# Reordering the front and the end of the state-space mixer of a three-part model kernel

## The reference, cut to what matters

```python
proj = hn @ w_in                                   # z 2048, xbc 3072, dt 64
z, xbc, dt_raw = jnp.split(proj, [SSD_INNER, SSD_INNER + SSD_XBC], axis=-1)
xbc = silu(depthwise_conv_centered(xbc, conv_w, conv_b))       # 5 taps over the tokens
xs, bm, cm = jnp.split(xbc, ...)                   # x 2048, B 4x128, C 4x128
dt = softplus(dt_raw.reshape(b, s, 2, 32) + dt_bias)
log_a = dt * -exp(a_log)                           # two directions, 32 heads
y = bidir_scan(cm, bm, xs * dt_f, xs * dt_b, log_a_f, log_a_b)  # chunks of 128
y = (y + xs * d_skip) * silu(z)
y = y * rsqrt(mean(y*y over each of 4 groups) + EPS) * norm_g
out = y @ w_out                                    # 2048 -> 1024
```

## Time and profile before

| | |
|---|---|
| median of 3 runs | 991.22 us (990.34 to 992.37) |
| profiled execution | 990.58 us, its span 988.2 us, mean granted TensorE clock 0.998 |
| TensorE (PE) busy | 954.5 us, 97% |
| ScalarE (ACT), VectorE (DVE), GpSimd (POOL) busy | 62%, 48%, 69% |
| DMA | 177.64 MB, mean 180 GB/s |
| the state-space mixer | about 342 to 548 us of the span |

### The profile page before, as it was taken

The page is one execution under the profiler, slowest core; times in us unless marked ns, Lnnn a source line. Parts: engine busy times, 40 slices in busy tenths (PEclk is TensorE's granted clock), DMA queues, the critical chain, the costliest instruction groups (busy, mean ns, idle before and its releaser), DMA issues. The chain is left out here.

```text
span 988.2 us, 15848 instructions
## 1 busy us (share of the span) xinstructions
PE 954.5 (97%) x6053; PEld 834.4 (84%) x6053; DVE 478.6 (48%) x1022; ACT 609.2 (62%) x1150; POOL 677.1 (69%) x538
## 2 busy tenths in 40 slices
PE   6999999999999999999998999999999999999998
PEld 5888768999999797888877799999997887788787
DVE  4734655444434545876844554444345231233652
ACT  7635668555455676977967764555566555775641
POOL 5986736857566686787778586657776964865664
PEclk9999999999999999999999999999999999999999
DMA  9684525775554657447456366565556538734221
GB/s 335 232 235 150 170 86 180 247 241 193 185 174 168 181 143 206 161 148 247 170 177 219 121 208 213 171 213 171 173 170 204 151 127 274 244 119 159 97 86 43
DMA packets 124952, 177.64 MB, mean 180 GB/s; under 512 B 13185, under 2 KB 86797, under 8 KB 124685
## 3 DMA queue, kind: packets, MB, share of 16 engines
q1 hardware_dynamic: 120701, 168.91, 52.4%
q10 hardware_dynamic: 4176, 7.71, 2.3%
HBM read 175.47 MB, written 5.24 MB: 183 GB/s over the span
## 5 line engine op out<-in xcount | busy, mean ns | idle before, releaser
L533 POOL TENSOR_TENSOR wlo<-raw,whi 128x512 fp32r<-128x512 f32 (+1 forms) x502 | 656.9, 1343 | 282.8 <-ACT whi L1254 266.8
L550 PE MATMUL PS<-Th,whi 128*128 128x256 f32 (+2 forms) x968 | 275.2, 285 | 0.8 <-DVE arena L1871 0.7
L552 PE MATMUL PS<-Th,wlo 128*128 128x256 f32 (+2 forms) x968 | 272.3, 282 | 0.0
L551 PE MATMUL PS<-Tl,whi 128*128 128x256 f32 (+2 forms) x968 | 272.3, 282 | 0.0
L1254 ACT ACTIVATE whi<-raw 128x1024 fp32r<-128x1024 f32 (+1 forms) x144 | 150.7, 1047 | 152.9 <-PE PS L552 113.7
L547 PE MATMUL PS<-whi,Th 128*128 128x512 f32 (+1 forms) x512 | 203.1, 397 | 10.1 <-DVE Tl L1848 7.3
L1871 DVE SCALAR_TENSOR_TENSOR arena<-PS,cols,arena 128x255 f32<-128x255 f32 (+1 forms) x272 | 118.6, 478 | 186.6 <-ACT arena L1388 160.9
L549 PE MATMUL PS<-whi,Tl 128*128 128x512 f32 (+1 forms) x512 | 197.1, 385 | 0.0
L548 PE MATMUL PS<-wlo,Th 128*128 128x512 f32 (+1 forms) x512 | 196.8, 384 | 0.0
L550 PEld LDWEIGHTS PS<-Th,whi 128*128 128x128 f32 (+2 forms) x968 | 184.0, 190 | 6.7 <-DVE arena L1871 3.1
L551 PEld LDWEIGHTS PS<-Tl,whi 128*128 128x128 f32 (+2 forms) x968 | 184.0, 190 | 1.8 <-issue 0.7
(11 more groups left out here) (250 smaller groups left out, 1034.6 us busy)
## 6 DMA issues: line engine op xcount, KB each, us to landing
raw<-in_ffn_w_up_dram SPq DMA_DIRECT2D x44, 1024.0 KB, 5.1
raw<-in_w_in_dram SPq DMA_DIRECT2D x23, 1024.0 KB, 5.3
raw<-in_ffn_w_down_dram SPq DMA_DIRECT2D x22, 1024.0 KB, 4.9
raw<-in_c_w_in_dram SPq DMA_DIRECT2D x16, 1024.0 KB, 5.3
raw<-in_ab_w_in_dram SPq DMA_DIRECT2D x14, 1024.0 KB, 7.4
raw<-in_c_w_out_dram SPq DMA_DIRECT2D x8, 1024.0 KB, 5.1
raw<-in_ab_w_out_dram SPq DMA_DIRECT2D x4, 1024.0 KB, 5.3
raw<-in_c_w_in_dram SPq DMA_DIRECT2D x8, 512.0 KB, 5.4
```

Source lines behind the costliest of these rows:

```text
L533: i = nc.gpsimd.tensor_tensor(lo_of(n)[:, c:e], raw[n % NRAW][:, c:e], hi_of(n)[:, c:e].bitcast(F32), ALU.subtract)
L550: mm(o, wh, ah, start=first, stop=False)
L551: mm(o, wh, al, start=False, stop=False)
L552: return mm(o, wl, ah, start=False, stop=last)
```

## The change

On TensorE, `dt_T` moves into the middle of the slot bc(0); `run_sums` moves from the middle of the second z slot to the middle of xs(0,1); the second z slot runs token tile by token tile, with a semaphore after the first; in `turned_x` of the first group the wait for the gate is by tile; `last_turn(1)` moves from before `out_last` into it, behind its first six products. On ScalarE, softplus comes ahead of the first centre taps with `ssd_rate` under the same Exp; the Ln, the exponential and the sums' copy come ahead of the last centre taps; weights' high parts move with them; the gate's SiLU runs by tile between the conv's SiLUs; in the last group one `high` goes behind the gate and one (`high(b + 5)`) ahead of `exps(4)`. On VectorE the softplus comes ahead of the first taps, its result stays in PSUM (`sp`) and is read there by the steps to `lnd` and `la`, with one more copy to SBUF. On GpSimd, in the last group, the first four `kept` come one slot earlier.

```diff
@@ -405,7 +405,8 @@
         sums_before, kept_before = {}, {}
         for g in range(SG):
             b = slot_no[(("bc", g + 1), 0)] if g + 1 < SG else slot_no[("mo1", 0)]
-            for u, k, m in ((0, 5, 4), (2, 5, 4), (4, 7, 5), (6, 7, 5)):
+            first = 4 if g + 1 < SG else 3
+            for u, k, m in ((0, 5, first), (2, 5, first), (4, 7, 5), (6, 7, 5)):
                 sums_before.setdefault(b + k, []).append((g, u))
                 kept_before.setdefault(b + m, []).append(8 * g + u)
@@ -986,8 +987,11 @@
                 def turned_x():
                     pe.wait_ge(*at("cv", (g, 1)))
-                    pe.wait_ge(*(at("s_m", (g - 1, 3)) if g else read((("z", 0), 1))))
+                    if g:
+                        pe.wait_ge(*at("s_m", (g - 1, 3)))
                     for t in range(NT):
+                        if not g:
+                            pe.wait_ge(*read((("z", 0), t)))
                         for j in range(4):
                             i = tr(PS[:, 4 + t, j * P:(j + 1) * P], cvb[:, j, t * P:(t + 1) * P], ident)
                     i.then_inc(*done("s_xt", g))
@@ -1042,7 +1046,6 @@
                 tile_diag(1)
                 if last:
                     ssd_slot(g + 1, 5, mid=lambda: last_turn(0))
-                    last_turn(1)
             def run_sums():
                 pe.wait_ge(*at("la"))
@@ -1055,17 +1058,26 @@
                         i = mm(PS[0:32, 7, P * k:P * k + P], dtt[:, 2 + c, 32 * r:32 * r + 32], cc(("le", "ge")[r]), start=True, stop=True)
                 i.then_inc(*done("sums"))
-            ssd_slot(0, 0)
-            pe.wait_ge(*at("dt_row"))
+            def steps_T():
+                pe.wait_ge(*at("dt_row"))
+                for t in range(NT):
+                    i = tr(PS[:, 7, S + 64 * t:S + 64 * t + 64], dtr[:, t * P:(t + 1) * P], ident[0:64, 0:64])
+                i.then_inc(*done("dt_T"))
+
+            ssd_slot(0, 0, mid=steps_T)
+            ssd_slot(0, 1)
+            ssd_slot(0, 2, mid=run_sums)
+            n = slot_no[(("z", 0), 1)]
+            pe.wait_ge(*low(n))
+            h, w = hi_of(n), lo_of(n)
             for t in range(NT):
-                i = tr(PS[:, 7, S + 64 * t:S + 64 * t + 64], dtr[:, t * P:(t + 1) * P], ident[0:64, 0:64])
-            i.then_inc(*done("dt_T"))
-            ssd_slot(0, 1)
-            ssd_slot(0, 2)
-            slot_tm((("z", 0), 1), 4, 4, False, True, mid=run_sums)
+                for k in range(4):
+                    i = three(PS[:, 4 + t, :], h[:, k * 512:(k + 1) * 512], w[:, k * 512:(k + 1) * 512],
+                              Th[:, 4 + k, t * P:(t + 1) * P], Tl[:, 4 + k, t * P:(t + 1) * P], False, k == 3, True)
+                i.then_inc(*(done("w_used", n) if t else done("sum", (n, 0, 1))))
             for g in range(SG):
                 ssd(g)
-            out_last("mo1", 8, (4, 6), by_tile=[("T_lo", ("yl", 0)), ("T_lo", ("yl", 1))])
+            out_last("mo1", 8, (4, 6), mid=lambda: last_turn(1), by_tile=[("T_lo", ("yl", 0)), ("T_lo", ("yl", 1))])
             ffn(1)
@@ -1409,13 +1421,19 @@
                 act.wait_ge(*at("t5_sum"))
                 act.dma_start(t5s.rearrange("(h k) -> h k", h=16), t5r).then_inc(*done("t5_src", 0, 16))
-            def softplus(key, neg, n):
+            def ssd_rate():
+                act.wait_ge(*at("load_ssd"))
+                act.activation(dtt[:, 5, :], dtt[:, 5, :], ACT.Exp).then_inc(*done("ssd_a"))
+
+            def softplus(key, neg, n, also=None):
                 spx = spxs[key]
                 act.wait_ge(*at("sp_x", key))
                 act.activation(spx[1], spx[0], ACT.Abs).then_inc(*done("sp_abs", key))
                 act.wait_ge(*at("sp_abs", key))
                 act.activation(spx[2], spx[1], ACT.Exp, scale=-1.0).then_inc(*done("sp_exp", key))
+                if also:
+                    also()
                 act.wait_ge(*at("sp_u", key))
                 act.activation(spx[4], spx[3], ACT.Ln).then_inc(*done("sp_ln", key))
@@ -1548,8 +1566,8 @@
                     act.activation(cvb[:, 2 * j + m, :], PS[:, xbc_bank(g, j), m * S:(m + 1) * S], ACT.Identity,
                                    scale=col("cw2", ch), bias=col("cb", ch)).then_inc(*done("c_ctr", (g, 2 * j + m)))
-            def ssd_silu(g):
-                for j in (2, 0, 1):
+            def ssd_silu(g, js=(2, 0, 1)):
+                for j in js:
                     act.wait_ge(*at("c_cnv", (g, j)))
                     act.activation(cvb[:, 2 * j:2 * j + 2, :] if j < 2 else bct[g % 2][:, :, :], cvb[:, 2 * j:2 * j + 2, :],
                                    ACT.Silu).then_inc(*done("cv", (g, j)))
@@ -1572,7 +1590,8 @@
                         i = act.activation(o, crow[v % 4][:, k, :], ACT.Exp, bias=ncs[:, a:a + 1])
                     i.then_inc(*done("s_e", (g, u)))
-                high(b + 1)
+                if more:
+                    high(b + 1)
                 if g:
                     act.wait_ge(*at("w_used", slot_no[(("z", g), 1)]))
                     copy_block(("z", g), zt[g % 2], 0, func=ACT.Silu)
@@ -1600,6 +1619,8 @@
                 exps(3)
                 if more:
                     ssd_centre(g + 1, 1, False)
+                else:
+                    high(b + 5)
                 exps(4)
                 exps(5)
                 high(b + 5)
@@ -1637,25 +1658,31 @@
                 act.wait_ge(*at("s_ss", (g, 1)))
                 sqrt_of(("s", g), st[:, 98:100], st[:, 96:98], 512)
+            def gate_tile(t):
+                act.wait_ge(*(at("w_used", slot_no[(("z", 0), 1)]) if t else at("sum", (slot_no[(("z", 0), 1)], 0, 1))))
+                act.activation(zt[0][:, t, :], PS[:, 4 + t, :], ACT.Silu).then_inc(*done("read_a", (("z", 0), t)))
+
             used(("dt", 0), ahead=False)
             act.activation(dtr, PS[0:64, 6, 0:S], ACT.Copy).then_inc(*done("dt_row"))
+            high(split_at(slot_no[(("bc", 0), 0)], 2))
+            softplus("ssd", False, 128, also=ssd_rate)
             ssd_centre(0, 2)
-            softplus("ssd", False, 128)
-            act.wait_ge(*at("load_ssd"))
-            act.activation(dtt[:, 5, :], dtt[:, 5, :], ACT.Exp).then_inc(*done("ssd_a"))
-            ssd_centre(0, 0)
-            ssd_centre(0, 1)
             act.wait_ge(*at("la"))
             act.activation(lnd, lnd, ACT.Ln).then_inc(*done("lnd"))
+            ssd_centre(0, 0, False)
+            high(split_at(slot_no[(("xs", 0), 0)], 3))
             act.wait_ge(*at("cums"))
             act.activation(dtt[:, 8:10, :], PS[:, 6, 0:128].rearrange("p (a b) -> p a b", a=2), ACT.Exp).then_inc(*done("ex"))
             act.wait_ge(*at("sums"))
             act.activation(csum, PS[0:32, 7, :], ACT.Copy).then_inc(*done("csum"))
             act.wait_ge(*at("csum"))
             act.dma_start(csr.rearrange("c r h t -> h (c r) t"), csum.rearrange("h (a t) -> h a t", a=4)).then_inc(*done("csr_out", 0, 16))
-            ssd_silu(0)
-            act.wait_ge(*at("w_used", slot_no[(("z", 0), 1)]))
-            copy_block(("z", 0), zt[0], 4, func=ACT.Silu)
+            ssd_centre(0, 1, False)
+            ssd_silu(0, (2, 0))
+            gate_tile(0)
+            ssd_silu(0, (1,))
+            gate_tile(1)
+            high(split_at(slot_no[(("xs", 0), 1)], 3))
             for g in range(SG):
                 ssd(g)
             post_norm(2, ("mo1", 7), "ffn1", 0)
@@ -2200,12 +2227,14 @@
                     last_scale(0)
                 ssd_tile(g, 1)
+            sp = spxs["ssd"][7]
+            softplus("ssd", 128, sp)
+            ts(lnd, sp, 1e-37, None, ALU.max)
+            nc.vector.tensor_copy(dtt[:, 0:2, :].rearrange("p a b -> p (a b)"), sp)
+            dve.wait_ge(*at("ssd_a"))
+            stt3(out=dtt[:, 2:4, :], in0=sp.rearrange("p (a b) -> p a b", a=2), scalar=-1.0, in1=bc(dtt[:, 5, :], 1, 2),
+                 op0=ALU.mult, op1=ALU.mult).then_inc(*done("la"))
             ssd_conv(0, 2)
-            softplus("ssd", 128, dtt[:, 0:2, :].rearrange("p a b -> p (a b)"))
-            ts(lnd, dtt[:, 0:2, :].rearrange("p a b -> p (a b)"), 1e-37, None, ALU.max)
-            dve.wait_ge(*at("ssd_a"))
-            stt3(out=dtt[:, 2:4, :], in0=dtt[:, 0:2, :], scalar=-1.0, in1=bc(dtt[:, 5, :], 1, 2), op0=ALU.mult, op1=ALU.mult)\
-                .then_inc(*done("la"))
             ssd_conv(0, 0)
             ssd_conv(0, 1)
             for g in range(SG):
```

## The result

The changed kernel takes 983.65 us (median of 5 runs), the kernel before 991.59 us beside it: the ratio is 0.9927, with a 95% interval of 0.9915 to 0.994, some 7.2 us less. The ratio leaves out one slow run of the kernel before (1006.54 us), and the two medians as they stand are 7.9 us apart. On another chip it measured 0.9921 (0.9903 to 0.994). The prediction was 984.2 us. The profiled execution took 984.40 us, with a span of 982.0 us and a granted clock of 0.998, as before.

A forecast was written before the change was run, and what follows sets the result against it. TensorE, busy 97% of the span, bounds the kernel, so only its waits count: -7.6 + 0.4 + 0.2 = -7.0 us on the profiled 990.58 gives 983.6, as a median 984.2. Range 982.8 to 987.8 us.

The forecast's parts named there:

- The six waits: TensorE's in the front, before the first output slot, `diag` of tiles 0 and 1, `last_turn(0)`, `last_turn(1)`: 7.62 us together.
- the higher price of a load: ScalarE's table switch in the front at 2.66 us with a drain, not 1.28: `la` some 2.8 us later, at 366.0.
- The thin margins: Front and last group: `ncs`, gate, s_yl and T_lo ready just before TensorE wants them; some 0.2 us to be lost.
- GpSimd's last low halves: Output projection's end: b+5, b+6, b+7 take 14.97 us behind the last `kept`; the last is late, 0.4 us comes back.
- a late `la`: Front: TensorE stands at `run_sums`, 3.6 us with the chain's old time, 985 to 988; at 378, 993.5; chance 0.04.
- the limit that the prediction had named: Last group: the forecast would be wrong if the row loads land over 5 us after issue.
- the rival with GpSimd's tail: Last group: a slower last row load delays three low halves, 986.2; with s_yl and T_lo late, 986 to 988; chance 0.2.
- The one on the other side: The slower rival, a late `la` in the front holding TensorE at `run_sums`; chance 0.04.
- the sign: Whole kernel: faster by over 0.2% at 0.90, within that at 0.06, slower at 0.04.

The follow-up runs named there:

- with `la` late: Changed kernel with `dt_T` and softplus back in their old places, `lnd` and `la` reading SBUF, `run_sums` still in mid xs1: 986.75 us, ratio 0.9942.
- the early high half alone: Changed kernel with only the high half of the next FFN's first slot moved between `last_root(1)` and `last_hi(1)`: 984.21 us, ratio 0.9919.
- the turn put back: Changed kernel with `last_turn(1)` ahead of the output projection's last pair again: 982.92 us, ratio 0.9874.
- the kernel with both edits: Changed kernel, VectorE making the output projection's last low half, next FFN's first high half between `last_root(1)` and `last_hi(1)`: 982.79 us, ratio 0.9894.
- front alone: Changed kernel with the edits of the last group and output projection undone, only the front's kept: 987.94 us, ratio 0.9957.

## Why the prediction came out, point by point

- **What bounds it.** That only TensorE's standing time counts held: its busy time did not change, and the waits that went, less the two that came, come to 6.83 us against the 6.78 measured.
- **The six waits.** Their sizes were read from start to start as 2.65, 0.86, 0.54, 2.02, 0.87 and 0.68, together 7.62; they gave 2.77, 0.86, 0.57, 2.05, 0.92 and 0.74, together 7.91. Most of the difference is the unwaited length that was subtracted: 1.58 and 1.73 us from the second group and 0.41 from a turn that had been waited for, where 1.51, 1.70 and 0.35 were reached. Each of the waits fell whole.
- **`la`.** Forecast at 363.2, it was there at 362.9 and wanted at 367.8. `lnd`, copy and `la` took 0.3 us each. That the trace loads four tables from Abs to the SiLUs, not six, held too, and the higher price of a load that the prediction gave beside its own, with `la` at 366.0, is not borne out: the ACTIVATE behind a load that ended at 358.35 us began at 358.36.
- **The thin margins.** `ncs`, the gate, s_yl and T_lo had 0.1 to 0.3 us each by the working and none was missed; the 0.2 us set aside for them was not needed.
- **GpSimd's last low halves.** Forecast as the next bound with 0.4 us; 0.61 was measured (0.44 of it recorded as idle). The last `kept`, forecast at 526.1, or 523.3 with the front's measured gain off, came at 523.31, and the three low halves took 15.01 us.
- **What was missed.** The prediction gave +0.4 for GpSimd and +0.2 for the margins; the runs have +0.61, another 0.11 as the products start up behind that wait, and, in the norm, where its sum did not look, +0.36: the residual add under GpSimd. The misses (0.3 us more gained, 0.5 more lost) partly cancel, so the stretch's 6.8 against the forecast 7.0 is closer than the terms. That the median came within 0.6 us of 984.2 is in part luck too: the profiled execution, for which the sum was made, was forecast at 983.6 and took 984.40, 0.8 us more.
- **What was credited wrongly.** 0.68 us were put down to moving `last_turn(1)`, and priced rightly as a wait; but putting the turn back costs nothing, since either place waits about as long, for the turn or for GpSimd. The term is right only together with the +0.4 behind it.
- **A sum in the rival.** For a late `la`, the prediction set the point where nothing is gained at 367.9 + 7.6 = 375.5. Its own net gain was 7.0, so it should have been 374.9. No run came near either.
- **The rivals.** The last row load took 5.0 us to land, right at the limit that the prediction had named, and ended in time for the forecast, so the rival with GpSimd's tail did not come up. The one on the other side was built: with `la` late, TensorE waits 1.5 us and not 3.6, as its old time held 1.97 us that depended on GpSimd running beside it. Even so it kept most of the gain, so the sign was never near.
- **The span.** It fell by 6.2 us where the stretch fell by 6.8, and the falls of the clock (last section) explain the gap. Each of the two profiles has one. That of the kernel before came at 752 us: from its product at 751.28 to its turns at 810.09 it took 58.81 us, and the changed kernel, with no fall there, took 58.20 for the same (744.31 to 802.51). That of the changed kernel came at 890: from its turns at 846.05 to the end it took 135.95 us, and the kernel before took 134.39 (853.81 to 988.2). So the one fall cost 0.6 us and the other 1.6. In the changed kernel's second profile the fall came where it had in the kernel before, and that span is 981.3 us, 6.9 less.

## What to carry to other kernels

Price a wait from start to start against the same work elsewhere in the trace, where it did not wait, and not by its recorded idle time: 0.71 us recorded were 0.92 here. When several waits in a row go, write down for every engine on the way when the next thing is wanted and when it is ready; the one that is late next (here GpSimd) decides what part of the sum stays. And look at what the helper engine's work now falls on: an engine freed earlier here stretched another engine's add by 0.6 us, and a reorder of two copies gave that back.

## What the hardware did that was not expected

**VectorE beside GpSimd.** VectorE's instructions that read only SBUF are longer while GpSimd runs: 0.23 against 0.78 and 1.08 us for a 128x128 scalar operation, 0.28 against 1.40 for the one with two tensors. With an operand in PSUM the same operations take 0.28 and 0.29 beside a running GpSimd. The Trainium skill, "SBUF — State Buffer", section Who interferes with whom, says that the two engines share one pair of ports under an exclusive lock, that a VectorE operation with two SBUF inputs contends with a GpSimd operation that reads SBUF, that a tensor_scalar in a two-port mode can contend too, and that whichever issues first has the pair for its whole instruction while the other is blocked. The trace agrees in which operations suffer (the numbers above). The size goes with the overlap: the residual add took 1.42 us where GpSimd overlapped it for none or 0.2 us, 1.47 and 1.49 with 0.3 (the early high half alone, and the turn put back), 1.99 with 0.8 and 2.56 with 2.0. GpSimd pays too: its four pieces took 5.03 us beside little of VectorE, 5.50 beside the longest add. The order fits as well. The changed kernel's add started inside a piece of GpSimd's and was held. In the kernel with both edits, VectorE's low half of 128x2048 had started at 535.88 and kept its 2.28 us, the time it took with GpSimd idle; GpSimd's first piece, from 536.77, took 2.55 us in place of 1.29. No run varied the order alone.

**The clock.** In 11 of the 14 profiled executions TensorE's granted clock falls once from 2.4 GHz to near the half of it, 1.2, for 3 to 4 us. In five it falls between 744 and 756 us, in four between 888 and 894, and in two inside the mixer (front alone, and the first run with `la` late). TensorE was busy without a pause from 886 to 890 us in one case (below) and for 62% of the 3.7 us before the fall in another (front alone). In the changed kernel's profile it is here (columns as above):

```profile
886.00:890.00 4.00, 4.00 (x46) 3.38 (x46) 2.69 (x12) 3.36 (x7) 1.95 (x2) 0.92 0.69 262
890.00:893.00 3.00, 3.00 (x9) 2.28 (x9) 1.29 (x8) 2.17 (x9) 3.00 (x3) 0.54 0.00 0
893.00:897.00 4.00, 4.00 (x23) 3.36 (x21) 1.77 (x6) 0.00 (x0) 0.22 (x1) 1.00 0.62 194
```

By the same kernel with and without one (30.43 against 28.93 us in the two runs with `la` late) it costs 1.5 us. At 890 us it cost 1.6, and at 752 only 0.6: there the changed kernel, with no fall, waits for 0.25 and 0.32 us (recorded) where the kernel before does not, so that part of the slower work fell into time in which TensorE would have stood. Differences of this size between whole times can come of it alone; the stretch of the changed kernel, 206.33 and 206.28 us in its two profiles, can be compared to a tenth where it holds no fall.
